# Prompt attention on one core: in small steps ScalarE's exponentials go ahead of its copies of turned tiles

## The reference, cut to what matters

```python
lg = jnp.einsum('bqghd,bwgd->bghqw', qs, k_win) + tab[t5_bucket(d_win)].transpose(2, 3, 0, 1)
p_win = masked_softmax(lg, m_win)
o_win = jnp.einsum('bghqw,bwgd->bqghd', p_win.astype(v_win.dtype), v_win)
return g[:, :, 0] * o_cmp + g[:, :, 1] * o_sel + g[:, :, 2] * o_win
```

## Time and profile before

| | us |
|---|---|
| median of 3 runs | 1485.69 |
| the runs, lowest and highest | 1485.40, 1486.38 |
| the profiled execution | 1483.41 |
| its span in the profile | 1481.6 |
| TensorE busy in it | 1421.1 (96%) |
| VectorE, ScalarE, GpSimd busy | 960.5, 704.1, 236.2 |
| attention stage, 740 to 1210: TensorE, VectorE, ScalarE busy | 449.7, 303.7, 352.0 of 470 |
| exponentials (L1897) in the stage | 256, 181.1 |
| copies of turned tiles (L1920, L1918) | 264 and 32, 149.6 and 9.0 |

### The profile page before, as it was taken

The page is one execution under the profiler, slowest core; times in us unless marked ns, Lnnn a source line. Parts: engine busy times, 40 slices in busy tenths (PEclk is TensorE's granted clock), DMA queues, the critical chain, the costliest instruction groups (busy, mean ns, idle before and its releaser), DMA issues.

```text
span 1481.6 us, 27910 instructions
## 1 busy us (share of the span) xinstructions
PE 1421.1 (96%) x10526; PEld 1225.8 (83%) x10526; DVE 960.5 (65%) x2309; ACT 704.1 (48%) x1546; POOL 236.2 (16%) x447
## 2 busy tenths in 40 slices
PE   4999999999999999989989989989999999999998
PEld 1889999999999999977767777777777766788886
DVE  2646878878787787767776576576666554643226
ACT  2332233332322323256677777777777756621111
POOL 1201020110101101131021242232231141000000
PEclk9899999999999999999999999999999999999999
DMA  9335733332333323597121321121121039963321
GB/s 343 109 107 113 123 116 87 93 92 61 108 80 93 104 49 108 133 338 247 60 94 32 74 73 44 45 78 44 39 58 30 22 112 346 279 205 100 90 85 36
DMA packets 169861, 164.76 MB, mean 111 GB/s; under 512 B 53756, under 2 KB 150268, under 8 KB 164352
## 3 DMA queue, kind: packets, MB, share of 16 engines
q1 hardware_dynamic: 153904, 94.11, 23.3%
q0 software_dynamic: 15824, 68.87, 15.2%
HBM read 131.27 MB, written 35.83 MB: 113 GB/s over the span
## 4 chain that ended last, share of the span: by engine, by line
PE 88%; DVE 4%; DMA 4%; ACT 2%; issue 2%; SPq 1%; POOL 0%; DVEq 0%; ACTq 0%
PE PS L1269 34%; PE PS L1636 12%; PE PS L1442 8%; PE PS L1407 7%; PE PS L1386 5%; PE PS L1387 4%; PE PS L1321 3%; PE PS L1226 2%; PE PS L1227 2%; PE PS L1228 2%; DMA adaw<-in_ada_w 1%; DMA kwb<-in_cache_k_win 1%; PE PS L1593 1%; PE PS L1433 1%; PE PS L1489 1%
## 5 line engine op out<-in xcount | busy, mean ns | idle before, releaser
L1269 PEld LDWEIGHTS PS<-bo,wsl 128*128 128x128 f32 x4104 | 499.4, 188 | 0.4 <-issue 0.4
L1269 PE MATMUL PS<-bo,wsl 128*128 128x264 f32 x4104 | 499.6, 284 | 0.0
L1897 ACT ACTIVATE pr<-PS,nm 128x640 f32<-128x640 f32 (+7 forms) x256 | 181.1, 709 | 44.6 <-DVE nm L2399 42.0
L1732 ACT ACTIVATE wsl<-wsum 128x512 fp32r<-128x512 f32 x105 | 65.6, 631 | 237.8 <-DVE wsum L2122 237.8
L1920 ACT ACTIVATE ptt<-PS 128x512 f32<-128x512 f32 x264 | 149.6, 601 | 43.1 <-PE PS L1407 42.9
L1407 PE MATMUL PS<-ident,pr 128*128 128x128 f32 x1056 | 147.2, 274 | 0.3 <-ACT ptt L1920 0.3
L1442 PE MATMUL PS<-ptt,kvt 128*64 128x256 f32 x1056 | 136.7, 390 | 0.0
L1407 PEld LDWEIGHTS PS<-ident,pr 128*128 128x128 f32 x1056 | 122.4, 141 | 9.2 <-issue 0.6
L1442 PEld LDWEIGHTS PS<-ptt,kvt 128*64 128x64 f32 x1056 | 66.9, 136 | 41.2 <-issue 16.5
L2399 DVE CUSTOM_DVE_ANT_0 PS<-PS,near,nm 128x256 f32<-128x256 f32 x192 | 94.7, 493 | 6.8
L2398 DVE TENSOR_REDUCE nm<-PS 128x1 f32<-128x128 f32 (+5 forms) x128 | 70.5, 551 | 39.6 <-PE PS L1387 38.9
(11 more groups left out here) (358 smaller groups left out, 2371.1 us busy)
## 6 DMA issues: line engine op xcount, KB each, us to landing
wr<-in_w_in SPq DMA_DIRECT2D x32, 512.0 KB, 5.5
adaw<-in_ada_w SPq DMA_DIRECT2D x8, 1024.0 KB, 10.0
wr<-in_w_in SPq DMA_DIRECT2D x32, 256.0 KB, 4.5
q_stacked<-qp POOLq DMA_DIRECT2D x64, 128.0 KB, 2.7
qb<-q_stacked SPq DMA_DIRECT2D x32, 256.0 KB, 3.1
mr<-mixed SPq DMA_DIRECT2D x16, 512.0 KB, 3.8
mixed<-yy POOLq DMA_DIRECT2D x16, 264.0 KB
xb<-in_x_prompt POOLq DMA_DIRECT2D x8, 512.0 KB, 4.3
```

Source lines behind the costliest of these rows:

```text
L1269: ins = pe.matmul(PS[:, 2 * q + c, 0:H // 2], w[:, x, kk, :], b[:, y, kk, c * H // 2:(c + 1) * H // 2], start=(first and kk == 0 and x == ...
L1897: act.activation(pr[r][:, h, 0:k], score_cols(b0, w), ACT.Exp, scale=-1.0, bias=nm[:, r, h:h + 1], accum_out=rsum[:, r, h:h + 1]).then_inc ...
```

## The change

In steps of at most four tiles, and in their first three quarters, the exponential of step w+2 is issued ahead of this quarter's copies of step w. In the last quarter, and in steps of five tiles or more, the order stays copies first. The small exponential and the copy of the table stay in front of both. The instructions themselves, what they wait for and what they signal are the same.

```diff
                     if w % 2 and h == 0:
                         copy_factors(w // 2)
+                    first = tiles_of(w) <= 4 and h < 3
+                    if first and w + 2 < NI:
+                        exps(w + 2, h)
                     for t in part:
                         copy_p(w, t)
-                    if w + 2 < NI:
+                    if not first and w + 2 < NI:
                         exps(w + 2, h)
```

## The result

| | before | after |
|---|---|---|
| timed, median of 22 runs each | 1486.53 us | 1489.87 us |
| lowest and highest | 1483.39, 1490.59 | 1487.31, 1494.29 |
| the profiled execution, its span | 1483.41, 1481.6 | 1489.76, 1487.9 |

The ratio is 1.0023, 95% interval [1.0016, 1.0029]: 2.4 to 4.3 us slower. The forecast was 1490.8 and 5.1 us slower, with a range of 1486.3 to 1493.4. The time lies in the range; the interval of the difference does not hold the 5.1.

What follows compares the result with a forecast made beforehand. TensorE, busy nearly the whole span, was taken as the bound. Later copies cost 3.86 + 1.26 = 5.12 us, earlier exponentials bring 0: 1488.5 for the profiled execution, 1490.8 on the runs' median scale, range 1486.3 to 1493.4.

Steps and rivals of the forecast that it cites:

- The chain of waits: Old profile's chain: through a copy in step 13 (from 845.35), then from TensorE through VectorE around 861, back at 868.98.
- the total of 39.1 us of waits: Attention stage: TensorE's scores wait for exponentials 38 + 24 times; the wait ending at 868.98 was to get no shorter.
- Earlier exponentials bring 0: About seven exponentials a pass gain up to 0.48 us each, none one TensorE waits for: 0, bounds 0 to -1.9.
- Step 12 to 13: Turning of step 13's first tile waits for step 12's third copy: 0.92 + 1.12 + 0.90 + 0.92 = 3.86 us slower.
- E + 2.12: Step 13's turning starts 2.12 us after E, the start of step 12's second exponential.
- Step 14: A copy behind its exponential delays the value matmuls by 0.42 us, in steps 14, 30 and 46: 1.26 us slower.
- The rest: Steps 0 to 3, their repeats and step 15: delayed copies cost 0; the wait at 866.05 takes in step 16's values.
- Absorbed: Rival: TensorE's lateness in steps 13 and 15 vanishes in the waits at 866.05 and 868.98; 1485.7, half absorbed 1488.3; 19%.
- the clock: TensorE's half-clock stretches, 2.24 us each: their place was taken not to depend on instruction order; one more or less possible.
- one less: Rival: one half-clock stretch of TensorE fewer than in the runs before, 1488.6; 12%.
- one more: Rival: one more half-clock stretch of TensorE, 1490.8 + 2.24 = 1493.0; 13%.

Runs made afterwards that it cites:

- the reverse edit: Kernel before, with the first tile's copy put behind the second exponential in steps 1, 17, 33 and 49: 1485.35 us against 1487.85, ratio 0.9987 [0.9977, 0.9998].

## Why the prediction was right, and what was off

*The chain of waits named the right place.* The old chain went through a copy in step 13. That the total of 39.1 us of waits on exponentials would not shrink held: it is 42.8.

*The time, 1490.8 against 1489.87:* nearer than the forecast earned. The kernel before has a median of 1486.53 over 22 runs, 0.84 above the three runs that the forecast was added to. The difference is the fairer test: 5.1 said, 3.3 measured.

*Earlier exponentials bring 0:* right. The other 38 places (steps 0 to 3 and 15 of each pass) changed nothing by themselves. The whole change and the reverse edit together show that the second exponential was the releaser, as worked out from the PSUM banks: moving only the first left the scores where they were, moving the second moved them.

*Step 12 to 13:* 3.86 said, 3.94 measured, with the slot-by-slot sequence (E + 2.12 said, 2.14 measured). One detail was missed: the turned table, which the prediction left aside, waits too, for the second copy (0.70 in its row), so that the wait shows as two rows, L1418 and L1407, and not as one of about 1 us on L1407. The sum is the third copy's either way.

*Step 14:* 1.26 said, 1.11 measured. The copy ran as said. But the prediction put the 0.14 us that lie between a copy's end and a turning also between a copy's end and the values; there it was 0.05 (859.97 to 860.02). Of this, 0.05 a time came back in the matmuls behind. The waits show this place only in part, as L1442 twice, 0.3 us in sum. *The rest:* 0, right. The wait at 866.05 did take in the values' 0.1: its idle time went from 0.50 to 0.36. TensorE, changed kernel:

```profile
868.82 0.45 PE L1386 MATMUL PS<-kwh,qb 128*128 128x384 f32 x1 [0.36 <-ACT pr L1897]
```

*Absorbed (19%):* fell, in the traces.

*The step that was off is the clock.* The prediction took as many stretches at 1.2 GHz after as before, as its likeliest case, and gave 12% to one less, which makes 2.9 us, inside the measured interval. The timed runs lose 1.9 us less (some 1.4 either way) to the lower clock than those of the kernel before. This term was put at 0; with -1.9 in its place the 5.1 becomes 3.2. It had named what may move a stretch, waits that come later in time, but took its place to be no property of the order of instructions, and so gave one more and one less alike (13% and 12%). At steps 17 to 19 the traces don't bear that out: three of four traces of the old order have it, none of three of the new one. The trace on which the forecast rested was also the luckiest of four: it had no stretch in the second pass (the earlier trace rows show its one in the fourth), the three later ones had one.

## What to carry to other kernels

On an engine that works in order, changing two instructions round pays only if the one that comes forward is the last thing another engine waits for; read that from the ring of buffers, not from the total of waits. An instruction that still has to wait should not stand in front of one that is ready: ScalarE idled 0.72 us with a finished tile behind it, and TensorE paid 0.9. Where timed runs and traces disagree by a us or two, compare the granted clock of the timed runs before looking for another mechanism.

## What was not expected of the hardware

The clock, above: in four traces, 1.3 us of lateness, whether waited or worked, went with a missing stretch at 1.2 GHz some 20 us later.

How soon TensorE goes on after a copy that it waited for: 0.14 to 0.15 us after the copy's end for the eight turnings of the changed kernel (L1418 and L1407), 0.05 for the three values rows (L1442). Why they differ is open.

A race of a few ns between VectorE and GpSimd, in step 16 of VectorE's list, while TensorE is in its step 17. It decides whether steps 17 to 20 take 20.6 or 20.0 us at the full clock: TensorE's step 17 is 0.58 us shorter in exactly the four of all 14 traces in which VectorE's multiply of 4 columns (L2431; L2434 in the changed kernel) is the short one. It took 0.74 us in the kernel before and 0.16 in one trace of the changed one. VectorE of the kernel before, then GpSimd of the same:

```profile
863.77 0.74 DVE L2431 TENSOR_TENSOR rg<-rrec,sg 128x4 f32<-128x4 f32 x1
```

```profile
863.76 0.73 POOL L1111 TENSOR_TENSOR mixs<-mixs,zau 128x256 f32<-128x256 f32 x1
```

and VectorE in the third trace of the changed kernel, where GpSimd's operation starts at 866.80 and takes 0.77:

```profile
866.81 0.16 DVE L2434 TENSOR_TENSOR rg<-rrec,sg 128x4 f32<-128x4 f32 x1
```

The rows, in steps of 10 ns, can't tell these two starts apart. In the traces' whole ns, VectorE starts 0 to 5 ns behind GpSimd in the four short cases and 6 to 11 in the ten long ones. Started further into GpSimd's multiply, VectorE's takes until that ends: in the old trace those that start 0.07, 0.15, 0.26 and 0.37 us after it take 0.68, 0.59, 0.48 and 0.37. The Trainium skill, "SBUF — State Buffer", section "SBUF: two separate sides", says that the two engines share a pair of ports which one instruction holds to its end, and that a VectorE operation with two inputs in SBUF blocks against a GpSimd one that reads SBUF. These rows agree.
